# One gather for U and V in the last two tiles of an expert layer

## The reference, cut to what matters

```python
experts = (i1 * PEER_N_KEYS + i2)          # 128 experts for each token: 8 heads x top 16
gates = jax.nn.softmax(best_s, axis=-1)    # (token, 128)

def expert_block(args):                    # a block of 128 tokens
    xt, e, g = args
    act = gelu(einsum('td,tkd->tk', xt, take(u_tab, e, axis=0))) * g
    return einsum('tk,tkd->td', act, take(v_tab, e, axis=0))
```

## Time and profile before

| | |
|---|---|
| median of three runs | 3177.84 us |
| the profiled execution | 3190.7 us |
| its span | 3188.9 us |
| TensorE busy | 1972.9 us (62%) |
| VectorE busy | 1669.3 us (52%) |
| ScalarE busy | 413.5 us (13%) |
| GpSimd busy | 1710.3 us (54%) |
| mean granted TensorE clock | 0.779 |
| moved by DMA | 1071.12 MB, mean 336 GB/s |
| of that by gathers | 805.40 MB |

### The profile page before, as it was taken

The page is one execution under the profiler, slowest core; times in us unless marked ns, Lnnn a source line. Parts: engine busy times, 40 slices in busy tenths (PEclk is TensorE's granted clock), DMA queues, the critical chain, the costliest instruction groups (busy, mean ns, idle before and its releaser), DMA issues.

```text
span 3188.9 us, 29288 instructions
## 1 busy us (share of the span) xinstructions
PE 1972.9 (62%) x9928; PEld 1140.5 (36%) x9928; DVE 1669.3 (52%) x4303; ACT 413.5 (13%) x1033; POOL 1710.3 (54%) x1540
## 2 busy tenths in 40 slices
PE   7999949798732255566775597889850012333465
PEld 3776437565400122334441255665620000000111
DVE  1223997712489974444216638752179995444200
ACT  2221123211100110111110112320100000000000
POOL 0000655334478866776446635433368887776664
PEclk9999869899955677777898798899975556555667
DMA  9864979788999999999989888878889999999897
GB/s 394 304 216 154 399 281 339 261 296 311 355 409 394 409 352 409 409 409 409 384 323 409 311 340 295 287 263 305 294 298 328 325 333 355 367 362 372 321 364 290
DMA packets 296211, 1071.12 MB, mean 336 GB/s; under 512 B 33408, under 2 KB 36352, under 8 KB 295296
## 3 DMA queue, kind: packets, MB, share of 16 engines
q0 software_dynamic: 221184, 805.40, 67.4%
q1 hardware_dynamic: 71712, 253.28, 21.3%
q10 hardware_dynamic: 3168, 10.55, 0.8%
HBM read 1065.80 MB, written 3.31 MB: 335 GB/s over the span
## 4 chain that ended last, share of the span: by engine, by line
PE 36%; POOL 24%; DVE 16%; issue 12%; DMA 7%; another core or an unknown queue 3%; ACT 1%; SPq 0%; ACTq 0%; DVEq 0%; POOLq 0%
POOL ring L1701 13%; POOL work L1701 11%; PE psum L853 8%; PE psum L842 6%; PE psum L771 6%; PE psum L1012 5%; DVE ring L1294 5%; DMA ring<-in_peer_v,v_experts 3%; PE psum L878 3%; PE psum L994 2%; DMA work<-in_peer_v,v_experts 2%; PE psum L955 1%; PE psum L979 1%; DVE work L1294 1%
## 5 line engine op out<-in xcount | busy, mean ns | idle before, releaser
L1701 POOL DMA_INDIRECT ring<-in_peer_u,experts x516 | 627.1, 1215 | 714.2 <-DVE experts L1504 316.7
L771 PE MATMUL psum<-ring,z 128*32 128x512 f32 x2000 | 436.6, 796 | 534.8 <-DMA ring<-in_peer_v,v_experts 371.5
L1701 POOL DMA_INDIRECT ring<-in_peer_v,v_experts x500 | 508.6, 1017 | 456.0 <-PE psum L771 266.5
L771 PE MATMUL psum<-work,z 128*32 128x512 f32 x1072 | 255.2, 840 | 291.0 <-DMA work<-in_peer_v,v_experts 166.5
L1294 DVE CUSTOM_DVE_ANT_0 ring<-ring,work 128x1024 f32<-128x1024 f32 x260 | 313.6, 1226 | 165.7 <-DMA ring<-in_peer_u,experts 159.3
L1294 DVE CUSTOM_DVE_ANT_0 work<-work 128x1024 f32<-128x1024 f32 x252 | 303.4, 1225 | 139.1 <-DMA work<-in_peer_u,experts 120.2
L1701 POOL DMA_INDIRECT work<-in_peer_v,v_experts x268 | 276.1, 1030 | 186.0 <-issue 77.4
L771 PEld LDWEIGHTS psum<-ring,z 128*32 128x32 f32 x2000 | 86.9, 131 | 771.6 <-issue 769.0
L1701 POOL DMA_INDIRECT work<-in_peer_u,experts x252 | 298.2, 1183 | 99.8 <-issue 73.8
L853 PE MATMUL psum<-work,wring 128*128 128x256 f32 (+1 forms) x1744 | 326.2, 346 | 4.4 <-issue 4.2
L1294 DVE CUSTOM_DVE_ANT_0 ring<-ring,h2a 128x1024 f32<-128x1024 f32 x256 | 304.6, 1220 | 15.3 <-DMA ring<-in_peer_u,experts 12.7
(11 more groups left out here) (187 smaller groups left out, 2348.5 us busy)
## 6 DMA issues: line engine op xcount, KB each, us to landing
wring<-in_wpack SPq DMA_DIRECT2D x380, 512.0 KB
ring<-in_wpack SPq DMA_DIRECT2D x88, 512.0 KB, 6.6
ring<-in_peer_u,experts POOLq DMA_INDIRECT x516
ring<-in_peer_v,v_experts POOLq DMA_INDIRECT x500
work<-in_peer_v,v_experts POOLq DMA_INDIRECT x268
work<-in_rows ACTq DMA_DIRECT2D x4, 1024.0 KB
work<-in_peer_u,experts POOLq DMA_INDIRECT x252
work<-in_rpb ACTq DMA_DIRECT2D x2, 1024.0 KB, 9.9
```

The source lines that it names most:

```text
L771: last = nc.tensor.matmul(psum[QUARTER * c:QUARTER * (c + 1), 6 + q, :], z[:, at:at + QUARTER], row(("v", n, o))[:, 512 * q:512 * (q + 1)] ...
L1701: pool.indirect_dma_start(row(key), None, a["peer_" + what], bass.IndirectOffsetOnAxis(ap=index, axis=0)).then_inc(got[ROW_CELL[key]], 16)
```

## The change

The last two tiles, 4 and 5 (`TOGETHER`), no longer sum by token.

- The host lays the U row and the V row of an expert side by side (`peer_uv`, 16384 rows x 2 layers of 8 KB). One gather, still by `experts`, brings both for 128 tokens: 128 rows of 8 KB, 1 MB. Token on partition in both halves. The turned indices and weights (`xi`, `xw`, `zf`) go for these tiles.
- 20 of the 21 cells make ten places of 8 KB (`PACKED`: five in `ring`, five in `work`). A place comes free when its V half has been summed.
- Work goes by steps of two experts (`PAIR`). `pd`: VectorE's two dots of the U halves. `pe`: ScalarE's GELU on the two. `pw`: ScalarE multiplies each by its gate. `pg`: ScalarE makes of each weight a 128 x 128 diagonal (identity times a weight for each partition). `pv`: TensorE multiplies the diagonal with the V half, two matmuls of 128 x 128 weights and 512 columns, into PSUM banks 6 and 7, over all 128 experts. In the program's step g stand `pv` of g-2, `pd` of g, `pe` of g-1, `pg` of g-2, `pw` of g-1.
- 46 of the 256 experts are summed by VectorE instead (`by_vector`: every fourth, from k = 64 on in tile 4 and from k = 8 on in tile 5), as V row times weight plus `pair_sum`, 128 x 1024; `fsum` adds that through the identity at the tile's end.
- `schedule`: the last 12 sum steps of tile 3 all stand beside `topk` groups 0 and 1 of tile 4, followed by `finish_items(3)`; 52 of the 128 pair steps lie beside the other six `topk` groups, the rest and the two finishes after the trunk.
- `diag`, `pair_sum` and the small vectors lie in the weight ring, which the trunk no longer uses then.

The core of the diff:

```diff
-TIGHT = (0, 3)
+TIGHT, TOGETHER = (0, 3), (4, 5)
+SMALL = 8
+PAIR = 2
+SUM_LAG = 2
+PACKED = RINGS // 2 + MORE // 2
...
+def by_vector(e):
+    k = e % KSEL
+    return k % 4 == 3 and k >= (SMALL if e >= KSEL else KSEL // 2)
...
+def pair_steps():
+    out, steps = [], len(TOGETHER) * PAIR_STEPS
+    for g in range(steps + SUM_LAG):
+        items = [("pv", g - SUM_LAG)] if g >= SUM_LAG else []
+        items += [("pd", g)] if g < steps else []
+        items += [("pe", g - 1)] if 0 < g <= steps else []
+        items += [("pg", g - SUM_LAG)] if g >= SUM_LAG else []
+        items += [("pw", g - 1)] if 0 < g <= steps else []
+        if g >= SUM_LAG and (g - SUM_LAG + 1) % PAIR_STEPS == 0:
+            items += finish_items(TOGETHER[(g - SUM_LAG) // PAIR_STEPS])
...
         two = PLACE[("topk", m + 1, 0, 2, 0)]
-        lay(flat(sums[20:26]), chosen, two)
-        lay(beside(next_dots, sums[26:], 6) + finish_items(n), two, PLACE[("begin", 2)] if m == 0 else end)
+        lay(flat(sums[20:26] if m == 0 else sums[20:]), chosen, two)
+        if m:
+            set_(finish_items(n), two)
+            steps = pair_steps()
+            for x, place in zip(steps, deal(two, end, steps[:PAIR_STEPS - SPARE])):
+                set_(x, place)
+            set_(flat(steps[PAIR_STEPS - SPARE:]), end)
+            continue
...
-            dots = dots_of(5)
-            set_(dots[:6] + turn(4) + beside(dots[6:], sums_of(4), 6) + finish_items(4), end)
-            set_(turn(5) + flat(sums_of(5)) + finish_items(5), end)
...
+                def add_pair(e):
+                    n, k = TOGETHER[e // KSEL], e % KSEL
+                    if k == 0:
+                        pe.wait_ge(sums_free, n)
+                    pe.wait_ge(got[ROW_CELL["uv", n, k]], 16 * ROW_USE["uv", n, k])
+                    pe.wait_ge(diags_made, SUM_NO[e] + 1)
+                    for q in range(2):
+                        last = nc.tensor.matmul(psum[:, 6 + q, :], diag[:, SUM_NO[e] % SMALL, :], pair_of_rows(n, k)[:, D + 512 * q:D + 512 * (q + 1)],
+                                                start=(k == 0), stop=False)
+                    last.then_inc(pairs_added, 1)
...
+                            nc.scalar.activation(diag[:, SUM_NO[e] % SMALL, :], ident, ACT.Identity,
+                                                 scale=pair_wts[:, e % SMALL:e % SMALL + 1]).then_inc(diags_made, 1)
...
+                    nc.vector.tensor_tensor_reduce(u, u, h2_of(t), 1.0, 0.0, ALU.mult, ALU.add,
+                                                   pair_dot[:, e % SMALL:e % SMALL + 1]).then_inc(pair_dots, 1)
...
+                        ins = nc.vector.scalar_tensor_tensor(out=pair_sum, in0=v_row, scalar=w, in1=pair_sum, op0=ALU.mult, op1=ALU.add)
...
+    out["peer_uv"] = cat([out["peer_u"], out["peer_v"]], 1)
```

More of the change, by code:

```diff
@@ L342, in schedule @@
         late = part(first, chosen, 0.65)
-        dots, sums, next_dots = dots_of(n), sums_of(n), dots_of(n + 1)
+        dots, sums = dots_of(n), sums_of(n)
+        next_dots = dots_of(n + 1)
         if m:
@@ L349, in schedule @@
         two = PLACE[("topk", m + 1, 0, 2, 0)]
-        lay(flat(sums[20:26]), chosen, two)
-        lay(beside(next_dots, sums[26:], 6) + finish_items(n), two, PLACE[("begin", 2)] if m == 0 else end)
[L352 to L361, removed]
-            dots = dots_of(5)
-            set_(dots[:6] + turn(4) + beside(dots[6:], sums_of(4), 6) + finish_items(4), end)
-            set_(turn(5) + flat(sums_of(5)) + finish_items(5), end)
+        lay(flat(sums[20:26] if m == 0 else sums[20:]), chosen, two)
[6 more added lines that the diff above has]
+            continue
+        lay(beside(next_dots, sums[26:], 6) + finish_items(n), two, PLACE[("begin", 2)])
+        dots = dots_of(2)
+        b = PLACE[("begin", 2)]
+        done = PLACE[("begin", 3)]
+        middle = part(b, done, 0.65)
+        lay(dots[:6] + turn(1) + beside(dots[6:], sums_of(1), 6) + finish_items(1), b, middle)
+        set_(turn(2), middle + 2)
+        lay(flat(sums_of(2)), middle + 3, done - 1)
+        set_(dots_of(3)[:8], done)
     return at
@@ L379, in program @@
         for g in range(HEAD_GROUPS):
-            assert where["topk", m, i, g, TOPK_PIECES - 1] < where["u", n, GROUP * g]
-    assert len(out) == len(WORK) + TILES * (KSEL + HEAD_GROUPS + 1 + FILLS + V_STEPS + 7)
+            first = ("u", n, GROUP * g) if n not in TOGETHER else ("pd", (KSEL * TOGETHER.index(n) + GROUP * g) // PAIR)
+            assert where["topk", m, i, g, TOPK_PIECES - 1] < where[first]
+    alone, together = TILES - len(TOGETHER), len(TOGETHER)
+    assert len(out) == len(WORK) + TILES * 7 + alone * (KSEL + HEAD_GROUPS + 1 + FILLS + V_STEPS) + together * (5 * PAIR_STEPS + 1)
     return out
@@ L778, in expert_work @@
                         add_rows(n, it[2])
+                    elif kind == "pv":
+                        for e in range(PAIR * n, PAIR * (n + 1)):
+                            if not by_vector(e):
+                                add_pair(e)
+                    elif kind == "fsum":
+                        pe.wait_ge(pairs_summed, sums_before(KSEL * (TOGETHER.index(n) + 1), True))
+                        for q in range(2):
+                            last = nc.tensor.matmul(psum[:, 6 + q, :], ident, pair_sum[:, 512 * q:512 * (q + 1)], start=False, stop=True)
+                        last.then_inc(pair_sums, 1)
+                    elif kind in PAIR_WORK:
+                        return
                     elif kind == "xw":
@@ L1311, in expert_work @@
                         return
+                    if kind in PAIR_WORK:
+                        if kind == "pv":
+                            for e in range(PAIR * n, PAIR * (n + 1)):
+                                if by_vector(e):
+                                    sum_pair(e)
+                        elif kind == "pd":
+                            for e in range(PAIR * n, PAIR * (n + 1)):
+                                dot_pair(e)
+                        return
                     l, t = EXPERT_TILES[n]
@@ L1686, in _ @@
                     m = [n_ for n_, (l_, ts) in enumerate(STAGES) if l_ == l and t in ts][0]
[L1687 removed]
+                    if what != "v":
                         if j % GROUP == 0:
```

122 lines of the change are left out of this document (103 added, 19 removed).

## The result

The change makes the kernel faster: **3067.09 us** (median of four runs, 3064.96 to 3068.39) against 3177.54 (four runs of the kernel before beside them, 3174.08 to 3179.76). The ratio is 0.9653, with a 95% interval of 0.9636 to 0.9669. The forecast was 3118 us. The side was right and the size was not: 51 us more were gained, and the time lies 13 us under the low end of the range. Rival 3 (the queue never drains, 3088 us) came nearest.

What follows compares the result with a forecast made beforehand. From 2640 us it took gather transfers, running below full rate, as the bound. 2436 + 655 + 3 + 5 + 6 + 24 = 3129 us of span, plus 1.8, minus 12.9, gave 3118 us; range 3080 to 3190.

Steps and rivals of the forecast that it cites:

- Rival 3: Last two tiles: deep 1 MB requests swallow the slow patches, transfers 630 us, the near tie costs nothing, 3088 us; chance 0.15.
- The start: Up to the first freed place, after tile 3's sums and finish: forecast at 2436 us, some 8 us of queue lost.
- 12.9 us to the median: Whole run: the profiled execution of the kernel before was 12.9 us above its runs' median, so the forecast subtracted that.
- The transfers: Pair gathers of tiles 4 and 5 after the start: 246 at 2.66 us (394 GB/s), 655 us before smaller additions.
- the near tie: Beside tile 4's `topk`: VectorE done at 2676 us against the 104th pair at 2686; 5 us added for mutual waits.
- the finish of tile 4: Between tiles 4 and 5: stops sums and dots for about 8 us of VectorE, 7 of TensorE; 6 us lost.
- slow patches: Pair gathers: a drop in transfer rate every 19.4 pairs, 12.7 times, at 2 us each, 25 us in all.
- full rate: Pair gathers: transfers unhindered at 409 GB/s, so 2.56 us for a pair of 1.049 MB.
- The tail: From the last landing to the end: last dot, GELU, weight, diagonal, pair sum, `fsum` and finish, 24 us.
- Rival 1: Pair gathers: scattered reading of HBM holds the rate at 353 to 360 GB/s, 3180 to 3194 us; chance 0.18.
- Rival 2: Pair sums (`pv`): TensorE at half clock is the bound, 3220 us, slower by 1.3%; chance 0.12.
- Rival 4: Beside `topk`: dots queue behind `topk` pieces, VectorE's 258 us turn into some 290, 3150 us; chance 0.05.

## Why the prediction was right on the side and wrong in the size

The span was forecast at 3129 us and was 3063.2. The 66 us, term by term:

**The start: 2436 forecast, 2415.8 measured, -20.** The timelines of the changed kernel (columns as in the earlier trace rows): TensorE's last sum step of tile 3, VectorE's first instruction of its finish, and GpSimd's first gather into a place that came free:

```profile
2389.29 1.92 PE L840 MATMUL psum<-ring,z 128*32 128x512 f32 x16 [1.80 <-DMA ring<-in_peer_v,v_experts]
```

```profile
2393.99 0.70 DVE L1475 TENSOR_TENSOR psum<-psum,acc 128x512 f32<-128x512 f32 x1 [38.36 <-ACT acc L1191]
```

```profile
2415.75 0.94 POOL L1860 DMA_INDIRECT work<-in_peer_uv,experts  x1 [17.36 <-PE psum L851]
```

The mechanism is the one forecast: VectorE stood for 38.4 us in front of the finish. But I had misread: the row at 2329.43 has 32 records, which are two steps, so the row at 2337.51 is the 22nd step and not the 21st. That is 6 us. This execution reached the same step at 2329.8, 7.7 us sooner than the one of before, which is chance and which the forecast took back in part with its 12.9 us to the median. A cadence of 5.95 in place of 6.1, a last step of 1.9 in place of 3.4, and 4 us less from the finish to the first place make up the rest.

**The transfers: 669 us forecast with the near tie, the finish of tile 4 and the last landing, 625 measured, -44.** This is the step that failed: its slow patches did not come, and its full rate was set too low. From 2415.8 to the last landing, at 3040.9:

```profile
3040.95 1.23 DVE L1425 CUSTOM_DVE_ANT_0 ring<-ring,work 128x1024 f32<-128x1024 f32 x1 [1.23 <-DMA ring<-in_peer_uv,experts]
```

- Full rate: "1.049 MB / 409 GB/s = 2.56 us". It is 2.49 us with 8 KB rows in a deep queue, 18 us less over 246 pairs. 409 was the highest stretch that I had read of before, all of rows up to 4 KB, and I had used it as a ceiling for rows that no gather there had.
- Slow patches: 12.7 times 2 us. None came, 25 us less. I had tied them to TensorE's records, by one interval of 28.8 us. The experiment with two gathers has these records unchanged and has the low rate back; what it adds is GpSimd's second request.
- The near tie, 5 us: VectorE was busy 171.7 of 200 us and waited for landings. The 104th dot ended at 2660 and not near 2690, and the last piece of `topk` ahead of it, at 2656.
- The finish of tile 4: 6 us forecast. The stretch 2720 to 2800 at 398 in place of 422 GB/s lost 4.5. The start of the pairs, 2400 to 2440 at 362, lost 5.7, of which 3.1 lie behind 2415.8 (368 GB/s up to 2440). The forecast had 8 for it, in its start.

Rival 3 had the mechanism right, a queue that never runs dry, and lacked the rate of the wider rows. It had 0.15 of the chance. It should have had more: that GpSimd needed 1.35 us for half a MB stood in the prediction itself, and I still kept two thirds of the patches' price beside it as if the queue had to run dry at them.

**The tail: 24 us forecast, 22.3 measured.** After the last landing: dot, GELU, gate and VectorE's last sum, `fsum` and the finish.

```profile
3042.86 5.39 PE L851 MATMUL psum<-work,wring 128*128 128x512 f32 x12 [1.55 <-ACT wring L1149]
3048.09 1.88 PE L866 MATMUL psum<-wring,consts 128*128 128x512 f32 x4
3051.94 0.70 DVE L1475 TENSOR_TENSOR psum<-psum,acc 128x512 f32<-128x512 f32 x1 [7.24 <-ACT acc L1191]
3060.11 0.33 SPq L809 DMA_DIRECT2D out<-x  x1
```

TensorE ran at its full clock (1.88 us for four records, where I had 3.4 at half), but had three experts to sum and not one.

**The rivals.** Rival 1, the rate stays at 353 to 360 because of scattered reading: false as it stood. Rows of 8 KB, chosen by the same scattered indices, move at 422, and scattered rows of 4 KB were 100 of the 123 MB that moved at 409. But U and V of an expert now lie side by side, so the reads are half as scattered as before; what of the 3% between 409 and 422 that is worth was not tried. Rival 2: false, by the change and by the experiment with nearly all sums on TensorE. Rival 4: false, VectorE kept 14% idle beside `topk`.

**Between span and median.** The forecast took 12.9 us off, since the profiled execution of before was that much over the median. The one of after was 2.1 us under its own. So 15 of the 66 us fall away again, and 51 are left.

## What to carry to other kernels

Where GpSimd gathers, count its requests before the bytes: when the issue of a request and the gap behind it come near to what the request's bytes take at full rate, the queue runs thin, and then it is slower even while it is busy. One request twice as wide costs GpSimd hardly more. Keep enough places for the ones that are held by the pipeline and for those in flight (with 1 MB each, some 3.5 in flight gave 393 GB/s here and 5.4 gave 416), and count what is held in items, by the lag in the program's order, and not in us.

A high busy share of the DMA engines is not a proof that memory is the limit: divide bytes by share times time, and compare with the best stretch. And what a ceiling is for one form of request must be left open for another.

## What the runs showed of the hardware that I had not expected

- Gathers of 128 rows of 8 KB held 420 to 422 GB/s over hundreds of us; with rows up to 4 KB the best long stretch had 409.
- The rate while busy went with the depth of the queue: 415 with ten places of 8 KB, 402 with eight, 369 with six; 374 and 375 with 4 KB rows that GpSimd could hardly issue fast enough.
- Taking four of ten places away cost 335 us, taking two away 39.
- A gather of 128 rows cost GpSimd 1.00 to 1.39 us in the mean of a stretch and 0.30 us before the next one, at 8 KB rows (1.21) hardly more than at 4 KB: two of 4 KB come to 2.74 us for an expert, more than its transfer takes.
- Idle times that the profile puts down to "issue" were waits for another engine: 33 of ScalarE ended 0.12 us after the start of the last READ_ACCUMULATOR of their dots, like the ones whose releaser is named.
